# A hybrid RWKV-7 and stick-breaking layer: spreading a head's attention loads over the groups, and the edge rows on GpSimd's queue

## What is computed

```python
for qs, qe in zip(starts, ends):          # 16 meta positions, then blocks of 128
    logits = einsum("bhqd,bhkd->bhqk", q[:, :, qs:qe], k[:, :, :qe]) * scale
    visible = arange(qe)[None, :] < arange(qs, qe)[:, None]      # strictly causal
    log_keep = where(visible, log_sigmoid(-logits), 0.0)
    log_between = cumsum(log_keep, axis=3, reverse=True) - log_keep
    weights = where(visible, exp(log_sigmoid(logits) + log_between), 0.0)
    outs.append(einsum("bhqk,bhkd->bhqd", weights, v[:, :, :qe]))
```

## Time and profile before

| | |
|---|---|
| median of three runs | 4381.3 us |
| profiled execution | 4379.16 us, its span 4377.4 us, so 1.8 us lie around the span |
| TensorE busy | 4171.0 us, 95% of the span |
| VectorE, ScalarE, GpSimd busy | 54%, 38%, 18% |
| mean granted TensorE clock | 0.977 of full |
| attention stage | from 2027 to 3104 us: TensorE busy 987.28 of 1077 us, VectorE 790.16 us |
| DMA in the attention stage | mean busy share of the 16 engines 0.38, 79 GB/s |

### The profile page before, as it was taken

How to read it: one execution, slowest core, us unless ns; L and a number is a source line. 1 busy time by engine, 2 the same in 40 slices (tenths; PEclk the granted TensorE clock), 3 DMA queues, 4 the chain that set the end, 5 groups by cost and what they waited for, 6 DMA issues and landing times. The chain is left out here.

```text
span 4377.4 us, 90822 instructions
## 1 busy us (share of the span) xinstructions
PE 4171.0 (95%) x35784; PEld 3344.7 (76%) x35784; DVE 2380.5 (54%) x3103; ACT 1666.2 (38%) x3296; POOL 804.4 (18%) x637
## 2 busy tenths in 40 slices
PE   7999999997999999997999999999899999999999
PEld 7888888985888888885555555655688888878887
DVE  5444444443444444442777777777467766743222
ACT  4222222223222222222666666666444444421111
POOL 2110111111111111110000000000256666610222
PEclk9999999998999999998999999999899999999999
DMA  2333433333333333334443442442233333355653
GB/s 93 109 117 119 122 109 110 102 115 110 109 118 116 109 104 118 107 103 113 89 94 69 82 93 63 87 94 62 75 114 99 101 104 100 92 184 177 189 188 129
DMA packets 486971, 479.74 MB, mean 110 GB/s; under 512 B 260610, under 2 KB 370818, under 8 KB 480914
## 3 DMA queue, kind: packets, MB, share of 16 engines
q1 hardware_dynamic: 475154, 450.33, 37.1%
q10 hardware_dynamic: 11520, 25.17, 1.6%
HBM read 305.45 MB, written 169.93 MB: 109 GB/s over the span
## 5 line engine op out<-in xcount | busy, mean ns | idle before, releaser
L1210 DVE TENSOR_TENSOR_SCAN kept<-keep,kept 128x512 f32<-128x512 f32 (+1 forms) x448 | 436.6, 975 | 63.1 <-ACT keep L1172 22.6
L1172 ACT ACTIVATE keep<-z 128x512 f32<-128x512 f32 (+3 forms) x704 | 343.4, 506 | 302.4 <-PE z L1105 242.1
L1636 POOL TENSOR_TENSOR off<-NT,tri 128x512 f32<-128x512 f32 x165 | 206.1, 1276 | 1181.6 <-ACT NT L1540 1181.6
L1115 PE MATMUL turned<-t_identity,kept 128*128 128x128 f32 (+1 forms) x2432 | 383.0, 280 | 38.6 <-DVE kept L1210 38.6
L1115 PEld LDWEIGHTS turned<-t_identity,kept 128*128 128x128 f32 (+1 forms) x2432 | 280.7, 136 | 154.9 <-DVE kept L1210 50.0
L1182 ACT COPY w<-turned 128x512 f32<-128x512 f32 (+4 forms) x704 | 363.2, 528 | 92.4 <-PE turned L1115 90.7
L1207 DVE TENSOR_TENSOR_SCAN kept<-keep,hidden 128x512 f32<-128x512 f32 (+3 forms) x256 | 284.2, 1116 | 156.3 <-ACT keep L1172 155.7
L1104 PE MATMUL z<-k_high,q_parts 128*128 128x512 f32 (+3 forms) x704 | 308.6, 439 | 36.1 <-DMA k_low<-scr_k_lo 27.9
L1142 PE MATMUL acc<-w,dv 128*64 128x512 f32 (+3 forms) x1280 | 322.8, 562 | 15.4 <-issue 15.4
L1104 PEld LDWEIGHTS z<-k_high,q_parts 128*128 128x128 f32 x704 | 137.8, 196 | 191.5 <-ACT keep L1172 107.6
L1105 PE MATMUL z<-k_low,q_parts 128*128 128x512 f32 (+3 forms) x704 | 256.6, 368 | 0.0
(11 more groups left out here) (554 smaller groups left out, 10688.4 us busy)
## 6 DMA issues: line engine op xcount, KB each, us to landing
w_raw0A<-in_w_main SPq DMA_DIRECT2D x42, 512.0 KB, 3.9
w_raw0B<-in_w_main SPq DMA_DIRECT2D x42, 512.0 KB, 3.9
w_raw1A<-in_w_main SPq DMA_DIRECT2D x41, 512.0 KB, 4.0
w_raw1B<-in_w_main SPq DMA_DIRECT2D x41, 512.0 KB, 3.8
KB<-scr_kb SPq DMA_DIRECT2D x33, 512.0 KB, 5.2
AR<-scr_ar SPq DMA_DIRECT2D x33, 512.0 KB, 5.4
y_raw<-scr_y SPq DMA_DIRECT2D x64, 256.0 KB, 4.5
merge<-scr_merge SPq DMA_DIRECT2D x64, 256.0 KB, 6.3
```

The lines of the kernel that those rows point to most:

```text
L1115: mm = pe.transpose(turned[num % TB][0:size, P * r:P * r + P], kept[kept_in(g)][:, src:src + size], t["identity"][:, :])
L1172: act.activation(keep[num % KB][:, 0:size], z[num % ZB][:, 0:size], ACT.Sigmoid, scale=-DH ** -0.5).then_inc(keep_done, 1)
L1210: dve.tensor_tensor_scan(dst, data, data, kept[kept_in(g)][:, end:end + 1], ALU.mult, ALU.bypass).then_inc(scanned, 1)
L1636: pool.tensor_tensor(out, a, b, op).then_inc(s[name], 1)
```

## The change

The ten loads of a head are no longer issued in a row. A table `due_after(g)` says which of them follow the store and the gate of group g, and the edge rows go to GpSimd's queue, with semaphores of their own. The diff, cut to its core:

```diff
+        def due_after(g):
+            pair, turn = divmod(g, 2 * GROUPS)
+            even, odd = 2 * pair + 2, 2 * pair + 1
+            if g == 0:
+                return [(odd, "queries"), (odd, "high")]
+            plan = {0: [(odd, "high")], 1: [(odd, "low"), (odd, "steps")], 2: [(odd, "diagonal")],
+                    3: [(even, "queries"), (even, "high")], 4: [(even, "low"), (even, "steps")], 5: [(even, "diagonal")],
+                    7: [(odd + 2, "queries")]}
+            return [(head, what) for head, what in plan.get(turn, []) if head < HEADS]
+
+        def free_after(head):
+            return GROUPS * (head - 1) if head % 2 == 0 else 2 * GROUPS * (head // 2) or 1
...
-                sp.dma_start(dv_diag[u][P - 1:P, tiles, :], edge[:, tiles, :]).then_inc(v_sem, 16)
+            def load_diagonal(head, first, last, done):
+                u, rows, tiles = head % 2, slice(DH * head, DH * head + DH), slice(first, last)
+                by_tile = scratch["dv"][CHUNK:TOK, rows].rearrange("(k p) c -> p k c", p=P)
+                sp.dma_start(dv_diag[u][0:P - 1, tiles, :], by_tile[0:P - 1, tiles, :]).then_inc(done, 16)
...
-            sp.dma_start(hidden[:, :], io["hidden"]).then_inc(const_in, 16)
             for p, (first, last) in enumerate(FIRST_PARTS):
-                load(0, first, last, qk_first[p], v_first[p])
-            load_gate(0)
-            load_gate(1)
+                load_queries(0, first, last, qk_first[p])
+                load_keys(0, first, last, k_high, "k_hi", qk_first[p])
+                load_keys(0, first, last, k_low, "k_lo", qk_first[p])
+                if p == 0:
+                    sp.dma_start(hidden[:, :], io["hidden"]).then_inc(const_in, 16)
+                load_steps(0, first, last, v_first[p])
+                load_diagonal(0, first, last, v_first[p])
+                if p == 0:
+                    load_gate(0)
+                    load_gate(1)
             for g in range(GROUPS_ALL):
                 sp.wait_ge(y_done, g + 1)
                 store_y(g)
                 if g + 2 < GROUPS_ALL:
                     load_gate(g + 2)
-                if g % (2 * GROUPS) == 0:
-                    head = head_of(g) + 1
-                    load(head, 0, QT, qk_in[head % 2], v_in[head % 2])
-                if g % (2 * GROUPS) == GROUPS - 1 and head_of(g) + 2 < HEADS:
-                    head = head_of(g) + 2
-                    load(head, 0, QT, qk_in[head % 2], v_in[head % 2])
+                for head, what in due_after(g):
...
-                    pe.wait_ge(v_in[head % 2], 64 * loads_of(head))
+                    pe.wait_ge(v_in[head % 2], 48 * loads_of(head))
+                    pe.wait_ge(edge_in[head % 2], 16 * loads_of(head))
...
+            for p, (first, last) in enumerate(FIRST_PARTS):
+                load_edges(0, first, last, edge_first[p])
+            for head in range(1, HEADS):
+                pool.wait_ge(y_done, free_after(head))
+                load_edges(head, 0, QT, edge_in[head % 2])
```

More of the change, by code:

```diff
@@ L987, in attention_phase @@
         qk_first, v_first = [[sem(f"a_{x}_first{b}") for b in range(len(FIRST_PARTS))] for x in ("qk", "v")]
+        edge_first, edge_in = [sem(f"a_edge_first{b}") for b in range(len(FIRST_PARTS))], [sem(f"a_edge_in{b}") for b in range(2)]
         qk_in, v_in = [sem(f"a_qk_in{b}") for b in range(2)], [sem(f"a_v_in{b}") for b in range(2)]
@@ L1026, in _, with load_queries, load_keys @@
+        def free_after(head):
+            return GROUPS * (head - 1) if head % 2 == 0 else 2 * GROUPS * (head // 2) or 1
         @block.sync
         def _(sp):
[L1028 to L1032, removed]
+            def load_queries(head, first, last, done):
+                u, rows, qs = head % 2, slice(DH * head, DH * head + DH), slice(P * first, P * last)
+                sp.dma_start(q_parts[u][0:DH, qs].bitcast(F32), scratch["q_hi"][rows, qs]).then_inc(done, 16)
+                sp.dma_start(q_parts[u][DH:P, qs].bitcast(F32), scratch["q_lo"][rows, qs]).then_inc(done, 16)
+            def load_keys(head, first, last, dst, name, done):
+                u, rows = head % 2, slice(DH * head, DH * head + DH)
@@ L1033, in load @@
                 k0 = P * first + (META if first else 0)
                 ks, src = slice(k0, P * last + META), slice(PAD + k0, PAD + P * last + META)
[L1035 to L1039, removed]
@@ L1040, in load, with load_steps @@
-                tiles = slice(first, last)
+                for part in (slice(0, DH), slice(DH, P)):
+                    sp.dma_start(dst[u][part, ks].bitcast(F32), scratch[name][rows, src]).then_inc(done, 16)
+            def load_steps(head, first, last, done):
+                u, rows, tiles = head % 2, slice(DH * head, DH * head + DH), slice(first, last)
                 by_tile = scratch["dv"][CHUNK:TOK, rows].rearrange("(k p) c -> p k c", p=P)
-                edge = scratch["v_edge"][:, rows].rearrange("(o k) c -> o k c", o=1)
@@ L1043, in load @@
                 if first == 0:
                     sp.wait_ge(cleared, 2)
-                    sp.dma_start(dv[u][0:META, 0, :], scratch["dv"][PAD:CHUNK, rows]).then_inc(v_sem, 16)
-                sp.dma_start(dv[u][:, first + 1:last + 1, :], by_tile[:, tiles, :]).then_inc(v_sem, 16)
-                sp.dma_start(dv_diag[u][0:P - 1, tiles, :], by_tile[0:P - 1, tiles, :]).then_inc(v_sem, 16)
-                sp.dma_start(dv_diag[u][P - 1:P, tiles, :], edge[:, tiles, :]).then_inc(v_sem, 16)
+                    sp.dma_start(dv[u][0:META, 0, :], scratch["dv"][PAD:CHUNK, rows]).then_inc(done, 16)
@@ L1050, in load_gate @@
+                sp.dma_start(dv[u][:, first + 1:last + 1, :], by_tile[:, tiles, :]).then_inc(done, 16)
+            def load_diagonal(head, first, last, done):
+                u, rows, tiles = head % 2, slice(DH * head, DH * head + DH), slice(first, last)
+                by_tile = scratch["dv"][CHUNK:TOK, rows].rearrange("(k p) c -> p k c", p=P)
+                sp.dma_start(dv_diag[u][0:P - 1, tiles, :], by_tile[0:P - 1, tiles, :]).then_inc(done, 16)
             def load_gate(g):
@@ L1067, in _ @@
                     load_gate(g + 2)
-                if g % (2 * GROUPS) == 0:
-                    head = head_of(g) + 1
-                    load(head, 0, QT, qk_in[head % 2], v_in[head % 2])
-                if g % (2 * GROUPS) == GROUPS - 1 and head_of(g) + 2 < HEADS:
-                    head = head_of(g) + 2
-                    load(head, 0, QT, qk_in[head % 2], v_in[head % 2])
+                for head, what in due_after(g):
+                    qk, v = qk_in[head % 2], v_in[head % 2]
+                    if what == "queries":
+                        load_queries(head, 0, QT, qk)
+                    elif what == "high":
+                        load_keys(head, 0, QT, k_high, "k_hi", qk)
+                    elif what == "low":
+                        load_keys(head, 0, QT, k_low, "k_lo", qk)
+                    elif what == "steps":
+                        load_steps(head, 0, QT, v)
+                    else:
+                        load_diagonal(head, 0, QT, v)
             for b in range(2):
@@ L1092, in value_steps @@
                 if head == 0:
-                    pe.wait_ge(v_first[min(rank(g), len(FIRST_PARTS) - 1)], 64 if rank(g) == 0 else 48)
-                else:
-                    pe.wait_ge(v_in[head % 2], 64 * loads_of(head))
+                    pe.wait_ge(v_first[min(rank(g), len(FIRST_PARTS) - 1)], 48 if rank(g) == 0 else 32)
+                    pe.wait_ge(edge_first[min(rank(g), len(FIRST_PARTS) - 1)], 16)
+                else:
+                    pe.wait_ge(v_in[head % 2], 48 * loads_of(head))
+                    pe.wait_ge(edge_in[head % 2], 16 * loads_of(head))
             def logits(g, qt, k0, size, num):
@@ L1227, in _, with load_edges @@
                 pool.memset(tile[:, :], 0.0).then_inc(cleared, 1)
+            def load_edges(head, first, last, done):
+                edge = scratch["v_edge"][:, DH * head:DH * head + DH].rearrange("(o k) c -> o k c", o=1)
+                pool.dma_start(dv_diag[head % 2][P - 1:P, first:last, :], edge[:, first:last, :]).then_inc(done, 16)
+            for p, (first, last) in enumerate(FIRST_PARTS):
[3 more added lines that the diff above has]
+                load_edges(head, 0, QT, edge_in[head % 2])
 LEVELS = [1, 4, 8, 16, 32]
```

## The result

The changed kernel takes 4627.3 us (median of 4 runs, 4621.1 to 4628.9) against 4382.0 us before (4 runs): 245 us longer, a ratio of 1.0558 with a 95% interval from 1.054 to 1.0577. The forecast was 4621 us in a range from 4555 to 4686. The profiled execution of the change has a span of 4627.1 us.

What follows compares the result with a forecast made beforehand. Attention was taken to run at TensorE's pace, busy 123.2 of 131 us per pair. Terms -59 + 122 + 153 + 31 - 7 = +240 us on 4379.2 gave 4619, plus 2.1 to the median: 4621 us, range 4555 to 4686.

Steps and rivals of the forecast that it cites:

- The reading it hung on: SyncE's loads: the 127-row load trickles through one DMA engine in 33.5 us and blocks whatever SyncE issues next.
- The load moved later: 127-row load behind turns 2 and 5 lands late; TensorE stalls 15.2 us (odd heads) and 21.9 us (even): +122, +153 us.
- Gates and stores: Turn 6's gate issued unblocked behind turn 4; VectorE's wait and TensorE's pauses go, 8.4 us per pair, seven times: -59 us.
- a store issue of some 32 us: Sign expected in the profile after: SyncE's store behind each 127-row load sits some 32 us in its issue.
- The clock: TensorE after each of fifteen stalls: some 5.5 us at half clock, 2.1 us lost each, +31 us.
- The start: Attention's start: gates 0 and 1 go behind the first part, removing the wait around the first gate: -7 us.
- The low keys: Keys' low part behind turn 1 arrives just in time: 0 us, bound up to 1 us for eight heads.
- the edge as the slow one: Rival: the one-row load itself needs the 34 us, so everything lands in time: 4315 us, chance 0.08.
- `dv` of 128 rows: Rival: this load, now behind turns 1 and 4, is the slow one: +78 us, 4459 us, chance 0.05.

Runs made afterwards that it cites:

- Experiment 6: Changed kernel with the 127-row load of heads 1 to 15 issued by GpSimd as four loads of four tiles: 4793.3 us, +414 us against the kernel before.
- experiment 3: Changed kernel with the 127-row load one turn earlier, behind turns 1 and 4: 4467.4 us, +90.7 us against the kernel before.
- experiment 4: Changed kernel with the 127-row load split into 48 and 79 rows: 4446.3 us, +69.7 us against the kernel before.
- experiment 2: Each half of the change alone, against the kernel before: edge rows on GpSimd 4364.5 us (-8.7); loads spread with edge rows on SyncE 4618.3 us (+245.1).
- experiment 1: 127-row load split into 112 and 15 rows: 4301.4 us in the changed kernel, 4297.5 us in the kernel before (-71.8 and -75.7 us).

## Why the prediction was right

**The reading it hung on** was that 127 rows go through one DMA engine, and that SyncE's next issue, whatever it is, waits for them. Splitting alone takes the 33.95 us out of an issue nobody touched. Moving the edge alone puts 34.20 us on a store. 79 rows block for 22.0 us rather than 33.8. All three are shown. Why the next issue has to wait at all, no run tells. The Trainium skill's page "DMA: Bandwidth & Descriptors", section "Why a DMA increments its semaphore by 16 and not by 1", takes the largest number up to 16 that divides the rows: one engine for 127 and for 79, 16 for 112 and 15 for 15. The runs agree that 127 and 79 rows are slow, at the share of about one engine (0.09 behind the 127 rows, 0.08 from 2470 to 2477 us behind the 79), and that 112 and 15 rows are not; how many engines serve those two they do not show. The same page's rule that another issuing engine saves only issue time (section "Issuing engines are not separate DMA queues") agrees as well: the edge's own issue is 0.54 us once no slow load is ahead of it, and the 33.95 were never its own. Experiment 6 does not agree with it: the 127-row load on GpSimd's queue cost more than a change of issue time, 447.1 us of pauses in place of 282.7. There the measurement decides.

**The load moved later** was +122 + 153 = +275 us, and the fifteen pauses measure 282.7. Those shown are 16.08 us for an odd head (forecast 15.2) and, at the next turn 0, 22.42 us for an even one (21.9). The term left out is small: from the gate product to the landing it is 38.3 us (2438.93 to 2477.19), not 37.4, because the blockade lasts 33.76 us from the load's issue, which I had as 0.41 + 32.5, scaled from a load a quarter as large. Experiments 3 and 4 move this term in two ways, by place and by size, and the time follows both within 3 us of what it gave.

**Gates and stores** were forecast at -59 us. The period of a pair, from the gate product of the second pair's turn 0 to that of the last one's, divided by six, is 130.5 us before, 123.1 with the split in the change: 7.4 us, against 8.4 forecast, so -52 for seven pairs. TensorE's busy time over these six periods is 737.5 us before and 720.9 with the split, 2.8 us a pair for the clock, where the forecast had 2.9. The gate's wait did go, as did the blocked issue's cost: the store of turn 3 sits 11.57 us in its issue, and nobody waits for it. The forecast had named "a store issue of some 32 us" as a sign. It is 11.57 and 23.92 us because the stores come due only 22.2 and 9.6 us after the load's issue.

**The clock** was forecast at +31 us, 2.1 for each pause. Two readings of the same six periods give less. The period of the change is 163.9 us, 40.8 longer than that with the split, and its twelve pauses sum to 228.6 us, 38.1 a pair. That leaves 2.7 us for two pauses. TensorE's busy time for the same instructions is 738.9 us in place of 720.9, or 3.0 a pair:

```profile
2241.31:3224.77 983.46, 738.89 (x4226) 460.35 (x4225) 594.12 (x624) 510.74 (x1105) 5.81 (x12) 0.88 0.30 65
2186.50:2924.95 738.45, 720.89 (x4227) 452.16 (x4226) 593.03 (x624) 508.74 (x1105) 5.81 (x12) 0.99 0.41 87
```

The first row is the change, the second the change with the split. So it is 1.4 to 1.5 us for each pause and 20 to 23 in all: this term was oversized by about 30%. The even head's pause in TensorE's timeline, and the windows row right behind the 16 us pause, which shows why the term is small:

```profile
2555.95 1.94 PE L1175 MATMUL acc<-w,dv 128*64 128x512 f32 x4 [22.42 <-issue]
```

```profile
2477.00:2483.00 6.00, 5.81 (x21) 3.02 (x22) 1.60 (x2) 2.06 (x4) 0.00 (x0) 0.65 0.94 212
```

The clock is 0.65 over these six us, which puts 4.2 us at the lower level (1.2 GHz) where I had 5.5, from a pause at the start of the stage. At 0.375 lost, 4.2 us cost 1.6. The cost does not follow from the length of the pause alone. TensorE is busy 739.2 us over the six periods of experiment 3 (pauses of 8.7 us on average), as long as in the change, and 744.7 in experiment 4 (7.6 us on average), which makes 2.0 us for each pause. Why, no run tells.

**The start** was forecast at -7 us, and the traces of experiment 2 give 7.8 less 0.7. One of its parts was off: gates 0 and 1 stand 8.73 us in their issue behind the first part's 127-row load, and TensorE's pause ahead of the second part's keys is 11.51 us in place of 8.92, so 2.6 longer where 1.2 was allowed. **The low keys** were taken at 0, with 1 us for each head as a bound. Two waits of TensorE for them behind 2100 us sum to 1.7 us.

The errors have both signs: +8 for the pauses, +7 for the gates, about -10 for the clock. That the total is only 6 us off is in part luck. The sign and the size rest on the pauses. The range has a slip: its terms sum to a lower end of 4559, and it was given as 4555. Both rivals fell: the edge as the slow one by experiment 2, `dv` of 128 rows by experiment 1, where it is left as it was and the slow stretch is gone.

The gain that one expects of such a spreading was not there to be had in this kernel. The ten loads in a row cost nothing by their number, as experiment 1 shows. They were early enough to hide 34 us of one slow load; spread out, they no longer were.

## What to carry to other kernels

When a DMA issue takes tens of us, look at the issue ahead of it in the same queue and at the bytes that move meanwhile, before moving the one that shows the time. Count a transfer's rows: 127 or 79 rows trickled, the 127 at one packet per 16.5 ns, 112 and 15 rows of the same data did not, and two issues in place of one made this kernel 1.7% faster. And before spreading loads to even out a queue, take for each load the time from its new place to its first use, and subtract the time that it needs to land. Where that is negative, the load has lost the cover that it had by being early, and the engine that uses it can stall by the difference.

## What the runs showed of the hardware that was not expected

- The split gave -75.7 us in the kernel before, where -66 was forecast. By the traces the pairs gave less than forecast (7.65 us each, so 54 in place of 59) and the start more. The gate product of the second pair's turn 0 comes 31.4 us earlier (2182.30 against 2213.71); less one pair's 7.65 and less the 1.7 us by which this stage began earlier, the start gave 22 us in place of 7. The loads of head 0's second and third parts had stood behind blocked issues of 7.33 and 7.72 us, which I had left in the sum as given, and gates 0 and 1 behind one of 19.94. With the split TensorE's pauses ahead of the second and third parts' keys are 3.07 and 0.72 us, where they were 8.92 and 6.81.
- A late gate of up to 12.3 us on VectorE costs nothing while TensorE waits for the next head's load meanwhile (experiment 3).
- On GpSimd's queue the same 127 rows kept the DMA engines busier (shares of 0.38 and 0.49 where it was 0.08) and were slower still: 16.7 us to land 127 KB, with GpSimd busy 4.6 us per issue.
- After a pause of 16 us TensorE's clock was at its lower level for 4.2 us and such a pause cost 1.4 to 1.5 us of the stage's time. Half of 4.2 would be 2.1, but a logits matmul at that level takes 0.80 us against 0.50 and not twice as long.
